# Two mixed tiles ahead of a layer's last units, and weights' loads ahead of stores, in a two-layer attention trunk

## The reference

```
for i in range(2):
    x = x + mixer_i(rms_norm(x, norm_i)) @ w_out_i
return rms_norm(x, final_norm)
```

## Time and profile before

| what | value |
|---|---|
| time, median of 3 runs | 1342.99 us (1341.93 to 1344.41) |
| the profiled execution's own time | 1341.48 us |
| its span, first to last instruction | 1339.7 us |
| mean granted TensorE clock | 0.988 of full |
| PE busy | 1280.8 us (96%) |
| DVE, ACT, POOL busy | 774.3, 637.2, 403.3 us (58%, 48%, 30%) |
| DMA | 97.29 MB, mean 73 GB/s |

### The profile page before, as it was taken

The page is one execution under the profiler, slowest core; times in us unless marked ns, Lnnn a source line. Parts: engine busy times, 40 slices in busy tenths (PEclk is TensorE's granted clock), DMA queues, the critical chain, the costliest instruction groups (busy, mean ns, idle before and its releaser), DMA issues.

```text
span 1339.7 us, 24582 instructions
## 1 busy us (share of the span) xinstructions
PE 1280.8 (96%) x8714; PEld 1190.7 (89%) x8714; DVE 774.3 (58%) x2337; ACT 637.2 (48%) x1767; POOL 403.3 (30%) x443
## 2 busy tenths in 40 slices
PE   5999999999899999999999999999999999988896
PEld 4998998987699999899989999899999899976896
DVE  5754453546571545566546765556766466676825
ACT  6444462545541444554446554455545465555111
POOL 2221151230351122212214822217622139313410
PEclk9999999999899999999999999999999999999998
DMA  5101022121455201110212211212310313123623
GB/s 199 38 17 48 25 64 72 33 79 53 139 158 197 95 24 52 37 26 19 55 49 66 82 56 35 64 36 81 97 31 18 86 56 78 55 81 97 189 95 126
DMA packets 101079, 97.29 MB, mean 73 GB/s; under 512 B 30688, under 2 KB 87520, under 8 KB 100960
## 3 DMA queue, kind: packets, MB, share of 16 engines
q1 hardware_dynamic: 100960, 95.73, 24.0%
HBM read 79.46 MB, written 16.25 MB: 71 GB/s over the span
## 4 chain that ended last, share of the span: by engine, by line
PE 87%; DVE 6%; ACT 2%; DMA 2%; issue 2%; SPq 1%; DVEq 0%; ACTq 0%
PE j_bank L1147 61%; PE o_bank L1286 7%; PE t_bank L1265 6%; PE s_bank L1252 5%; PE j_bank L1230 3%; PE s_bank L1254 2%; DVE ht_lo L1774 1%; PE s_bank L1147 1%; DMA w_raw<-in_w_out 1%; PE o_bank L1147 1%; DMA gate<-in_positions 1%; DVE xr L1764 0%; ACT probs L1379 0%; DVE probs L1611 0%; DVE w_lo L1575 0%
## 5 line engine op out<-in xcount | busy, mean ns | idle before, releaser
L1147 PE MATMUL j_bank<-w_hi,ht_hi 128*128 128x384 f32 (+1 forms) x1328 | 451.6, 340 | 18.4 <-DVE ht_lo L1774 9.0
L1147 PE MATMUL j_bank<-w_hi,ht_lo 128*128 128x384 f32 (+1 forms) x1328 | 439.4, 331 | 0.0
L1147 PE MATMUL j_bank<-w_lo,ht_hi 128*128 128x384 f32 (+1 forms) x1328 | 439.4, 331 | 0.0
L1147 PEld LDWEIGHTS j_bank<-w_hi,ht_hi 128*128 128x128 f32 x1328 | 252.5, 190 | 30.9 <-issue 25.0
L1018 POOL TENSOR_TENSOR w_lo<-w_raw,w_hi 128x768 fp32r<-128x768 f32 (+1 forms) x60 | 110.0, 1834 | 494.9 <-ACT w_hi L1370 494.2
L1147 PEld LDWEIGHTS j_bank<-w_lo,ht_hi 128*128 128x128 f32 x1328 | 253.1, 191 | 0.0
L1147 PEld LDWEIGHTS j_bank<-w_hi,ht_lo 128*128 128x128 f32 x1328 | 252.6, 190 | 0.0
L1379 ACT ACTIVATE probs<-probs,stat 128x256 f32<-128x256 f32 (+1 forms) x512 | 230.9, 453 | 43.6 <-DVE stat L1616 42.0
L767 ACT COPY probs_t<-t_bank 128x256 f32<-128x256 f32 (+1 forms) x128 | 57.9, 452 | 298.2 <-PE o_bank L1286 292.5
L1370 ACT ACTIVATE w_hi<-w_raw 128x768 fp32r<-128x768 f32 (+1 forms) x120 | 88.1, 763 | 85.6 <-PE j_bank L1147 48.2
L1608 DVE CUSTOM_DVE_ANT_0 probs<-s_bank,masks 128x256 f32<-128x256 f32 x224 | 86.1, 421 | 58.0 <-PE t_bank L1265 57.4
(11 more groups left out here) (169 smaller groups left out, 1868.6 us busy)
## 6 DMA issues: line engine op xcount, KB each, us to landing
w_raw<-in_w_qkv SPq DMA_DIRECT2D x64, 384.0 KB, 3.6
coef<-coef_dram SPq DMA_DIRECT2D x96, 128.0 KB, 3.0
w_raw<-in_w_gate SPq DMA_DIRECT2D x32, 256.0 KB, 3.4
mix_dram<-xr SPq DMA_DIRECT2D x12, 512.0 KB, 3.9
w_raw<-in_w_out SPq DMA_DIRECT2D x16, 384.0 KB, 3.7
qk<-mix_dram SPq DMA_DIRECT2D x12, 512.0 KB, 4.4
xr<-in_x SPq DMA_DIRECT2D x8, 512.0 KB, 7.2
out<-xr SPq DMA_DIRECT2D x8, 512.0 KB, 2.7
```

The source lines that it names most:

```text
L1147: last = pe.matmul(to, a(x_, kt), b(y_, kt), start=(start and kt == kts[0] and x_ == y_), stop=(stop and kt == kts[-1] and x_ == 1))
```

## The change

The four edits act in both layers, except where the kernel has stores (layer 0 alone).

- The last step's second gate piece moves from unit 2 to unit 4.
- Tiles 0 and 1 are copied by ACT in the last pair but one, once PE is through the first half of the last gate piece. DVE splits tile 0 there, ahead of its own copy of that gate piece, and tile 1 in the last pair. PE runs row blocks 0 to 3 of both tiles in the last pair; row block 6 and then 4 and 5 of both follow the last `times_v`, and the last coefficients' turn stands behind them.
- Behind the units, ACT does the weights' quarters 2 and 3, the last even turn, the last coefficients' exponential, tiles 2, 3 and 4, the SiLU, and tile 5. DVE does `coefs_last` right behind `store_ot`, then tile 2, the copy of the coefficients, tiles 3 and 4, the weights' split, the first `end_mix`, tiles 5 and 6, the second `end_mix`, tile 7. POOL does its weights' split ahead of both `end_mix` calls.
- In the output parts SP issues the weights' loads that follow the next part's splits ahead of the finished part's store and the residual load. A load still waits for the low part that frees its half.

```
--- before.py
+++ after.py
@@ -80,7 +80,7 @@
             _slots.append((JOBS[-1], _at))
         if _s.ends_group:
             JOBS.append(("gate", _layer, _s.g))
-            _slots.append((JOBS[-1], [0, 2, 8, 12] if _s.last else [12, 13, 14, 15]))
+            _slots.append((JOBS[-1], [0, 4, 8, 12] if _s.last else [12, 13, 14, 15]))
         for _job, _pieces in _slots:
             for _k, _slot in enumerate(_pieces):
                 if _slot is None:
@@ -971,8 +971,9 @@
                     wait_end_mixed(sp, 1, 1)
                     sp.dma_start(gain_row, final_norm.rearrange("(o d) -> o d", o=1).broadcast_to([P, D])).then_inc(gain_in, 16)
                 for c in range(OUT_PARTS):
-                    raws_after(splits_of("job", layer, c) + splits_of("mid-job", layer, c))
+                    raws_after(splits_of("mid-job", layer, c))
                     if c + 1 < OUT_PARTS:
+                        raws_after(splits_of("job", layer, c + 1))
                         if layer == 0:
                             x1_store(c, range(NB), x1_out)
                         if c + 2 < OUT_PARTS:
@@ -1109,9 +1110,9 @@
                                 rotate_two(s.t + 1, k // 4, k // 2 % 2)
                         for b, k in mixes_at(s, slot):
                             mix(b, k)
-                end_mix(steps[-1], 0)
                 w_lo(END_SPLIT[layer])
-                end_mix(steps[-1], 1)
+                for n in range(2):
+                    end_mix(steps[-1], n)
                 for c in range(OUT_PARTS):
                     w_lo(splits_of("job", layer, c) + splits_of("mid-job", layer, c))
                 if layer == 0:
@@ -1333,16 +1334,17 @@
                         if END_TURN in pair and s.last:
                             coef_turn(s, 0)
                         if a == UNITS - 2 and s.last:
-                            early_rows(layer, 0, EARLY_ORDER[:FRONT_ROWS])
+                            for kt in range(2):
+                                early_rows(layer, kt, EARLY_ORDER[:FRONT_ROWS])
                 last = steps[-1]
                 for u in range(UNITS - TURN_BACK, UNITS):
                     turn(last, u)
                 for u in range(UNITS - V_BACK, UNITS):
                     times_v(last, u)
-                early_rows(layer, 0, EARLY_ORDER[FRONT_ROWS:])
-                early_rows(layer, 1, EARLY_ORDER[:FRONT_ROWS])
+                for rows in ([6], [4, 5]):
+                    for kt in range(2):
+                        early_rows(layer, kt, rows)
                 coef_turn(last, 1)
-                early_rows(layer, 1, EARLY_ORDER[FRONT_ROWS:])
                 for kt in range(2, MIX_LOADS):
                     early_rows(layer, kt, EARLY_ORDER)
                 for r in range(2):
@@ -1509,11 +1511,12 @@
                             empty_turn(b, u)
                         for item in front:
                             fill_hi(*item[1:])
-                        if a == UNITS - 2 and s.last:
-                            act.wait_ge(piece_full, PIECE.filled(last_piece(JOB[("gate", layer, GROUPS - 1)])))
-                            mix_in_split(layer, 0)
                         for slot in pair:
                             exps(s, slot)
+                        if a == UNITS - 4 and s.last:
+                            act.wait_ge(half_done, JOB[("gate", layer, GROUPS - 1)] + 1)
+                            for k in range(2):
+                                mix_in_split(layer, k)
                         if SILU_AT in pair and before is not None and before.ends_group:
                             silu(before)
                         if END_COEF in pair and s.last:
@@ -1532,14 +1535,14 @@
                             if slot == (1 if layer == 0 else 3) and before is not None and before.ends_group:
                                 den_exp(before, 0)
                 last = steps[-1]
-                for k in range(1, MIX_LOADS):
+                w_hi(END_SPLIT[layer])
+                empty_turn(last, UNITS - 2)
+                den_exp(last, 1)
+                act.wait_ge(piece_full, PIECE.filled(last_piece(JOB[("gate", layer, GROUPS - 1)])))
+                for k in range(2, MIX_LOADS):
                     mix_in_split(layer, k)
-                    if k == 1:
-                        den_exp(last, 1)
-                        empty_turn(last, UNITS - 2)
-                    if k == 2:
+                    if k == 4:
                         silu(last)
-                        w_hi(END_SPLIT[layer])
                 for r in range(2):
                     wait_end_mixed(act, layer, r)
                     mix_split(layer, MIX_LOADS + r, ot[out_region(last)][:, r, :])
@@ -1913,7 +1916,7 @@
                         for slot in pair:
                             mask_max(s, slot)
                         if a == UNITS - 2 and s.last:
-                            mix_split(layer, 0, mix_in[0])
+                            mix_split(layer, 1, mix_in[1])
                         if END_COEF in pair and s.last:
                             coefs_first(s, 0)
                         b, u = unit_before(s, a + 1, TURN_BACK)
@@ -1928,6 +1931,8 @@
                             store_ot(b, u // NB, (u % NB) // 4)
                         for slot in pair:
                             w_lo(SLOT_SPLIT.get((s.t, slot), []))
+                        if a == UNITS - 4 and s.last:
+                            mix_split(layer, 0, mix_in[0])
                         for item in rest:
                             if item[0] == "fill":
                                 fill_lo(*item[1:])
@@ -1949,18 +1954,18 @@
                 coefs_first(last, 1)
                 empty_turn(last, UNITS - 1)
                 store_ot(last, 1, 1)
-                for k in range(1, MIX_LOADS):
+                coefs_last(last, 1)
+                for k in range(2, MIX_LOADS):
                     mix_split(layer, k, mix_in[k % 3])
-                    if k == 1:
-                        coefs_last(last, 1)
+                    if k == 2:
                         coef_copy(last, 1)
-                    if k == 2:
+                    if k == 4:
                         w_lo(END_SPLIT[layer])
-                    if k == 3:
                         end_mix(last, 0)
-                mix_split(layer, MIX_LOADS, ot[out_region(last)][:, 0, :])
-                end_mix(last, 1)
-                mix_split(layer, MIX_LOADS + 1, ot[out_region(last)][:, 1, :])
+                for k in range(2):
+                    mix_split(layer, MIX_LOADS + k, ot[out_region(last)][:, k, :])
+                    if k == 0:
+                        end_mix(last, 1)
                 for c in range(OUT_PARTS):
                     if c == 0:
                         w_lo(splits_of("mid-job", layer, c))
```

## The result

| | median | all runs | profiled run, span |
|---|---|---|---|
| before | 1342.46 us | 1341.57 to 1344.41 | 1341.48, 1339.7 |
| after | 1331.46 us | 1326.98 to 1332.38 | 1332.38, 1330.6 |
| after, run again beside the experiments | 1330.04 us | 1327.45 to 1331.77 | 1331.77, 1330.0 |

The ratio of after to before is 0.9909, 95% interval [0.9884, 0.9935]; in the second set 0.9898 [0.9877, 0.9919]. The medians put the gain at 11.0 and 13.3 us where 13.5 was forecast. The runs of the changed kernel lie up to 5.4 us apart.

A forecast was written before the change was run, and what follows sets the result against it. TensorE (PE) was taken to bound the kernel (87% of the chain), through its idle and lower-clock time. Terms 7.2 + 3.5 + 2.1 + 0.7 = 13.5 off 1341.48, plus 1.5, gave 1329.5 us; own range 1327 to 1332, with rivals 1322.5 to 1337.5.

The forecast's parts named there:

- A: Layer 0's output projection start: two tiles in front bring tile 2 8.0 us earlier, tile 7 1 us late; gain 7.2 us.
- C: Layer 1's end: tile 7 4.1 us earlier, minus 2.0 of clock loss; gain 2.1 us, bounds -1.5 and 11.1.
- D: Last group, both layers: gate piece from second to third pair; gain 0.6 us in layer 1, 0.1 in layer 0.
- B: Layer 0's output parts: weights' loads ahead of stores remove PE's 1.84 us wait and 1.7 clock loss; gain 3.5 us.
- The first two go, since tile 0 is ready: Layer 1's end: PE's 2.93 us idle and the 1.7 us clock loss would vanish.
- Moved at nothing: Edits priced at zero: ACT's weights' copies ahead of the last softmax turn, and coefficient steps behind the last turn.
- R1: Rival: PE alone sets the end in both layers; 18.1 us gain, or 1324.9; chance 0.20.
- R2: Rival: DVE and POOL block each other, head start lost at tile 7; layer 1 -1.0; 7.5 gain, 1335.5; chance 0.22.
- R3: Rival: in layer 0 the weights' load still lands late, sharing queues with residual loads; 10.0 gain, 1333.0; chance 0.06.
- R4: Rival, slower: POOL stretches layer 1's DVE row from tile 2's split to the last to 40 us; about 1355; chance 0.03.

The follow-up runs named there:

- the kernel with the second head pair by DVE: Changed kernel, but in layer 1 DVE makes all end products of the second head pair in whole rows of 1024, POOL none: 1324.85 us.

## Why the prediction was right, and where it was not

The time and the sign came out as forecast. The mechanism did for layer 0 and not for layer 1.

That the time came so near is in part luck. In the pair of profiled executions A gave 0.9 us more than its term, C 3.4 and D 1.4 less and the rest 0.6 less, so that these two gained 9.1 us and not 13.5. The medians gave 11.0 and 13.3, of a kernel whose runs lie 5.4 us apart.

**A, right, 0.9 too small.** From pair 14 to tile 7 the two traces with the old order take 42.3 and 42.0 us, and those with the new one 34.1 to 35.7. Tile 2 started at 364.91 (365.4 forecast), after one wait of 0.61. Tile 7 waited 0.60 against the 1 us forecast, and no lower clock followed, where 0.7 was put down. I had charged a clock loss to a wait shorter than any that shows one in my rows. No run separates A's own parts, the two tiles in front and the SiLU behind tile 4.

**B, right: 3.5 and 3.5**, the loads landing in 3.2 and 4.6 us where 4 to 5 was forecast. What the forecast did not have is that the clock part of it (1.7 in the sum, 1.4 between the traces) is not certain: the same wait without the lower clock is worth 2.1.

**C, the failed step: 2.1 forecast, -1.3 measured, -0.5 by the means of seven traces.** Two sentences fail. "The first two go, since tile 0 is ready": the idle time of 2.93 before 1226.40 went from tile 0 and came back as 1.37 and 2.15 at the turn and tile 2, with 6.8 us at 0.50 behind them where 3.80 us at 0.56 stood. And, of what "Moved at nothing" lists, "The coefficient steps behind the last turn: PE has rows 4 to 6 of both tiles in front, 18 matmuls or 3.1 us": the steps took 3.9 us and the split behind them 2.42. I had measured the cover, and priced what it covers at its undisturbed duration, though C moved POOL's products to just that moment. Without those products there, in four of the kernels above, the steps take 1.4 us and the split 1.2, and PE does not wait at tile 2. PE's wait of 3.48 us at tile 7 lies in the 3 to 6 that the prediction named. But tile 7 came 1.1 us earlier relative to the pair, not 4.1; the clock loss behind it was forecast at 2.0 and is 2.4.

**D, 0.7 forecast, about 0.8 by the stages (1.1 in layer 0, -0.3 in layer 1) and 2 to 4 by the medians.** The sum was near, the places were not: in layer 1 the wait of 2.19 us at 1178.07 came exactly as forecast, but the clock fell for longer behind it (0.66 over 10 us, or 0.83 in the kernel with the second head pair by DVE). In layer 0 I looked for clock loss in one trace that had none; two of the four traces with the old place have it.

**The rivals.** R1 (PE alone) holds nearly for layer 0 and not for layer 1. R2's mechanism, each engine blocking the other, is what happens in layer 1, and its -1.0 there is near what was measured (-1.3 and -0.5), though two of the three waits come at the turn and tile 2 and not at tile 7; in layer 0 the two engines stretch each other too (split 6 took 2.72 us at 374.52 and split 5 2.00), but PE waited no more than 0.60 us for it, and so the time stayed with the forecast. The Trainium skill's rule (SBUF — State Buffer, "SBUF: two separate sides"), an exclusive lock for the whole instruction, agrees with the 1.41 us of a 0.18 us addition beside POOL's 1.54 us addition. I had it in the text and gave it to a rival, where it should have priced C. The 7.00 us of POOL's weights' split, which the prediction takes as bearing the rule out, is more than one such stop: DVE ran four operations in a row beside it (2.00, 0.94, 1.98 and 0.67 us from 371.33 on), and the same split takes 1.84 us at 356.64 of the changed kernel. R3 fell (no wait, the loads in 3.2 and 4.6 us). R4 fell: DVE's row from tile 2's split to the last ran 27 us (1224.82 to 1251.99), not 40.

**Open.** Why the runs of the changed kernel spread over 5.4 us is not settled. Its profiled runs have the lower clock at different places (at 544.0 in the first trace and not in the second). The stage up to layer 1's pair 2 takes 710.3 to 713.2 us over the thirteen traces, whatever the edit, so its -0.8 above tells nothing of the change.

## What to carry to other kernels

Before you give GpSimd a share of VectorE's work to shorten VectorE's row, add up what each of its instructions costs VectorE when they meet: here up to 1.2 or 1.3 us for a product that VectorE makes in 0.54 to 0.69 us, and handing six of them back was worth more than the whole reordering of layer 1's end. When a chain of short operations is moved behind new cover, look at what runs on the other engine in the moment to which it is moved, and price it at the disturbed duration. And read a change of place in every stage that it touches, over several traces: one trace of layer 1 gave D as a whole the wrong sign.

## What the runs showed of the hardware

- A VectorE operation with two operands in SBUF that meets a GpSimd elementwise operation is longer by up to about the latter's whole duration: 1.41 us for 0.18, 1.35 for 0.16, 2.42 for 1.22. GpSimd's are stretched as well: 2.17 to 2.39 for 1.3 to 1.5. A copy from PSUM (0.69) and a reciprocal (0.25) beside such operations kept their durations.
- Equal waits on TensorE are not followed by equal clock: 1.84 us idle, then 4.57 us at 0.63 before; 1.88 us idle, then 4.57 us at 1.00 without B.
- A product over 1024 columns takes VectorE 1.23 us and two over 512 take 1.41.
- The place of a load in one DMA queue sets when it lands: 384 KB took 10.75 us behind a 1.5 MB store and two loads of 0.75 MB, and 3.2 and 4.6 us ahead of them.
